# The last chunk of an expert that fills several: high and low row parts side by side as one stationary block

## What is computed

```python
    flat_e = e_idx.reshape(-1)
    order = jnp.argsort(flat_e)
    tok = order // TOP_K
    sizes = jnp.bincount(flat_e, length=N_EXPERTS).astype(jnp.int32)
    xs = t[tok].astype(w_gate.dtype)
    hid = jax.nn.silu(lax.ragged_dot(xs, w_gate, sizes)) * lax.ragged_dot(xs, w_up, sizes)
    y = lax.ragged_dot(hid, w_down, sizes)
```

## Time and profile before

| | us |
|---|---|
| median of 3 runs | 2054.48 |
| lowest and highest | 2053.87, 2055.65 |
| the profiled execution | 2051.71 |
| its span, first to last instruction | 2049.9 |
| PE busy in the span | 1758.5 (86%) |
| DVE busy | 1289.9 (63%) |
| ACT busy | 965.6 (47%) |
| chunks of layer 0, first matmul of the first to first of the last | 680.0 to 1013.2 |
| chunks of layer 1, the same | 1680.2 to 1995.3 |

### The profile page before, as it was taken

The page is one execution under the profiler, slowest core; times in us unless marked ns, Lnnn a source line. Parts: engine busy times, 40 slices in busy tenths (PEclk is TensorE's granted clock), DMA queues, the critical chain, the costliest instruction groups (busy, mean ns, idle before and its releaser), DMA issues. The chain is left out here.

```text
span 2049.9 us, 40296 instructions
## 1 busy us (share of the span) xinstructions
PE 1758.5 (86%) x15365; PEld 1449.2 (71%) x15366; DVE 1289.9 (63%) x1849; ACT 965.6 (47%) x1492; POOL 200.1 (10%) x261
## 2 busy tenths in 40 slices
PE   3998988999697799999919988899996959999992
PEld 0898677788554688888818986888883548888882
DVE  1388255566445796886653882656663368999674
ACT  2254522233312786886432445323332248888651
POOL 0000022222000100000020000212220000000001
PEclk7999999999798899999969999999997979999996
DMA  7221094330323898997642210431004069999854
GB/s 317 72 83 44 9 366 145 129 130 5 72 86 152 311 391 334 345 397 284 227 170 78 77 44 17 163 126 54 2 3 147 31 236 387 402 394 400 351 205 164
DMA packets 112110, 376.64 MB, mean 184 GB/s; under 512 B 14730, under 2 KB 35490, under 8 KB 86374
## 3 DMA queue, kind: packets, MB, share of 16 engines
q1 hardware_dynamic: 83310, 303.85, 39.7%
q10 hardware_dynamic: 20168, 39.89, 5.1%
q0 software_dynamic: 8496, 30.94, 4.0%
HBM read 332.87 MB, written 41.78 MB: 183 GB/s over the span
## 5 line engine op out<-in xcount | busy, mean ns | idle before, releaser
L1967 DVE TENSOR_TENSOR expert_w_lo<-shared,expert_w_hi 128x2048 fp32r<-128x2048 f32 x192 | 430.5, 2285 | 49.2 <-ACT expert_w_hi L1909 48.7
L1909 ACT ACTIVATE expert_w_hi<-shared 128x2048 fp32r<-128x2048 f32 x192 | 361.0, 1915 | 43.8 <-PEq L143 40.6
L1851 PE MATMUL ps<-expert_w_hi,expert_x_hi 128*128 128x512 f32 x592 | 232.0, 392 | 6.3 <-DVE expert_x_lo L1963 6.3
L1853 PE MATMUL ps<-expert_w_hi,expert_x_lo 128*128 128x512 f32 x592 | 231.8, 392 | 0.0
L1852 PE MATMUL ps<-expert_w_lo,expert_x_hi 128*128 128x512 f32 x592 | 231.7, 391 | 0.0
L1851 PEld LDWEIGHTS ps<-expert_w_hi,expert_x_hi 128*128 128x128 f32 x592 | 112.2, 190 | 30.5 <-issue 7.1
L1853 PEld LDWEIGHTS ps<-expert_w_hi,expert_x_lo 128*128 128x128 f32 x592 | 112.0, 189 | 23.4
L1852 PEld LDWEIGHTS ps<-expert_w_lo,expert_x_hi 128*128 128x128 f32 x592 | 112.0, 189 | 23.2
L1887 PE MATMUL ps<-expert_w_hi,expert_hid_hi 128*128 128x512 f32 x296 | 118.7, 401 | 1.0 <-ACT expert_hid_hi L1941 0.2
L1013 POOL TENSOR_TENSOR mixer_NTb<-mixer_Bt,consts_sb 128x256 f32<-128x256 f32 x120 | 88.6, 762 | 282.0 <-DVE mixer_Bt L1288 215.2
L1888 PE MATMUL ps<-expert_w_lo,expert_hid_hi 128*128 128x512 f32 x296 | 115.5, 390 | 0.0
(11 more groups left out here) (342 smaller groups left out, 3700.6 us busy)
## 6 DMA issues: line engine op xcount, KB each, us to landing
shared<-in_w_gate SPq DMA_DIRECT2D x64, 1024.0 KB, 7.2
shared<-in_w_up SPq DMA_DIRECT2D x64, 1024.0 KB, 8.8
shared<-in_w_down SPq DMA_DIRECT2D x64, 1024.0 KB, 9.1
qkv<-in_w_ada SPq DMA_DIRECT2D x20, 1280.0 KB, 6.0
shared<-in_w_in SPq DMA_DIRECT2D x10, 2048.0 KB, 7.9
y_table<-expert_y ACTq DMA_DIRECT2D x37, 512.0 KB, 8.8
qkvT<-in_w_ada SPq DMA_DIRECT2D x20, 768.0 KB, 8.3
y_table<-zero ACTq DMA_DIRECT2D x1, 12800.0 KB, 50.8
```

The source lines that it names most:

```text
L1851: pe.matmul(bank, hi, w_hi[:, j, w], start=first, stop=False)
L1853: return pe.matmul(bank, lo, w_hi[:, j, w], start=False, stop=last)
L1909: act.activation(w_hi[:, j, :], raw[:, j, :], ACT.Copy).then_inc(w_hi_done, 1)
L1967: dve.tensor_tensor(w_lo[:, j, :], raw[:, j, :], w_hi[:, j, :].bitcast(F32), ALU.subtract).then_inc(w_lo_done, 1)
```

## The change

A last chunk with at most 64 rows, of an expert that has others before it, takes a path of its own (`full` is false there). The 64 high and the 64 low parts of its rows are set side by side as one stationary block of 128 (`x_both`), and two products (with `w_hi` and with `w_lo`) take the place of three. The upper and lower halves of the result then have to be added: the gate product by two copies of ACT and an addition of DVE ahead of Silu, the hidden rows by the transposing matmul itself (against two stacked identities, `eye`), the output by two copies of ACT and two additions of DVE. The same is done for the hidden rows (`hc`, a view of `hid_hi`). To make `x_both`, ACT and DVE each make one more instruction in chunks that have another behind them.

Which path is taken is computed in the router (`R.full`, one number for each expert), loaded by a fourth value load of each engine, and tested by two branches: one ahead of the full code, one ahead of the new code. All experts pass these, those with one chunk too.

```diff
@@ tail_phase, PE and DVE
-                for t in range(NT):
-                    for u in range(t + 1):
+                for t in range(NT + 1):
+                    n = min(t + 1, NT)
+                    for u in range(n):
...
+                ch.link(dve.tensor_tensor(tmp2[:, 4, :], G.ps[:, BX, NT * NE:(NT + 1) * NE], tmp2[:, 0, :], ALU.subtract))
+                ch.link(dve.tensor_scalar(tmp2[:, 4, :], tmp2[:, 4, :], float(HC - P), None, ALU.is_gt))
+                dve.scalar_tensor_tensor(out=R.full[:, :], in0=tmp2[:, 0, :], scalar=1.5 * P, in1=tmp2[:, 4, :], op0=ALU.is_lt, op1=ALU.max)
@@ for_experts, all engines
+                full = eng.value_load(R.full[0:1, bass.ds(e, 1)], min_val=0, max_val=1)
...
-                chunk(e, eng.value_load(R.last[0:1, bass.ds(e, 1)], min_val=0, max_val=MAXC - 1), True, final)
+                k = eng.value_load(R.last[0:1, bass.ds(e, 1)], min_val=0, max_val=MAXC - 1)
+                with eng.If(full > 0):
+                    chunk(e, k, True, final, True)
+                with eng.If(full < 1):
+                    chunk(e, k, True, final, False)
@@ expert_phase, PE
+                def half_product(bank, rows, j, w, first, last):
+
+                    pe.matmul(bank, rows, w_hi[:, j, w], start=first, stop=False)
+                    return pe.matmul(bank, rows, w_lo[:, j, w], start=False, stop=last)
...
+                        if not full:
+                            if q % HQ == 0:
+                                pe.wait_ge(h_lo_done, k * 2 + (q // HQ + 1))
+                            for h in range(2):
+                                w = slice(q % 2 * D + h * 512, q % 2 * D + (h + 1) * 512)
+                                mm = half_product(G.ps[:, 5 + h, :], both(hc, q), j, w, q == 0, q == KF - 1)
@@ ACT
-                    act.activation(sg[:, :], G.ps[:, 0, :], ACT.Silu).then_inc(sg_done, 1)
+                    if full:
+                        act.sem_inc(gc_done, 1)
+                    else:
+                        act.activation(sg[lower, :], G.ps[upper, 0, :], ACT.Copy)
+                        act.activation(sg[upper, :], G.ps[lower, 0, :], ACT.Copy).then_inc(gc_done, 1)
+                        act.wait_ge(gs_done, k + 1)
+                    act.activation(sg[:, :], G.ps[:, 0, :] if full else sg[:, :], ACT.Silu).then_inc(sg_done, 1)
...
+                        for h in range(2):
+                            act.activation(y[lower, h * 512:(h + 1) * 512], G.ps[upper, 5 + h, :], ACT.Copy).then_inc(yc_done, 1)
@@ DVE
+                    if full:
+                        dve.sem_inc(gs_done, 1)
+                    else:
+                        dve.wait_ge(gc_done, k + 1)
+                        dve.tensor_tensor(sg[:, :], sg[:, :], G.ps[:, 0, :], ALU.add).then_inc(gs_done, 1)
                     next_lo(0)
...
+                        for h, done in enumerate((ya, yd)):
+                            dve.wait_ge(yc_done, k * 2 + (h + 1))
+                            dve.tensor_tensor(y[lower, h * 512:(h + 1) * 512], y[lower, h * 512:(h + 1) * 512], G.ps[lower, 5 + h, :],
+                                              ALU.add).then_inc(done, 1)
```

More of the change, by code:

```diff
@@ L1766, in expert_phase @@
         y = ph.sb("y", [P, D])
+        xc = ph.sb("x_both", [P, KD, 2, HC], F32R)
+        hc = h_hi[:, :].rearrange("p (q a n) -> p q a n", q=KF, a=2)
         cur = ph.sb("cur_idx", [P, 1], I32)
@@ L1771, in expert_phase @@
             ph.sem(n) for n in "picked g_p u_p xt_p ht_p y_p half_used w_hi_done w_lo_done".split())
-        sg_done, hid_done, x_hi_done, x_lo_done, h_hi_done, h_lo_done, ya, yd, y_out, passed = (
-            ph.sem(n) for n in "sg_done hid_done x_hi_done x_lo_done h_hi_done h_lo_done ya yd y_out passed".split())
+        gc_done, yc_done, gs_done, sg_done, hid_done, x_hi_done, x_lo_done, h_hi_done, h_lo_done, ya, yd, y_out, passed = (
+            ph.sem(n) for n in "gc_done yc_done gs_done sg_done hid_done x_hi_done x_lo_done h_hi_done h_lo_done ya yd y_out passed".split())
         gathered = ph.dma_sem(G.soft["gathered"])
         turned = G.ps[:, 2:4, :].rearrange("p b n -> p (b n)")
+        turned_q = turned.rearrange("p (q n) -> p q n", n=P)
         HQ = KF // 2
+        lower, upper = slice(0, HC), slice(HC, P)
         def half_of(a, m):
@@ L1857, in _, with chunk @@
                 turn(0, 0, KD)
-                def chunk(e, k, last, final):
+                def chunk(e, k, last, final, full):
                     pe.wait_ge(x_lo_done, k + 1)
@@ L1867, in chunk @@
                             at = slice(q * P, (q + 1) * P)
-                            mm = product(G.ps[:, n, :], x_hi[:, at], x_lo[:, at], j, q % 4 * FF, q == 0, q == KD - 1)
+                            if full:
+                                mm = product(G.ps[:, n, :], x_hi[:, at], x_lo[:, at], j, q % 4 * FF, q == 0, q == KD - 1)
+                            else:
+                                mm = half_product(G.ps[:, n, :], both(xc, q), j, slice(q % 4 * FF, q % 4 * FF + FF), q == 0, q == KD - 1)
                             if last and q == 3:
@@ L1902, in _, with take @@
             def _(act):
-                def take(k):
+                def take(k, last):
                     act.wait_ge(xt_p, k + 2)
                     act.wait_ge(u_p, k + 1)
+                    if not last:
+                        act.activation(xc[:, :, 0, :], turned_q[:, :, 0:HC], ACT.Copy)
                     act.activation(x_hi[:, :], turned, ACT.Copy).then_inc(x_hi_done, 1)
@@ L1951, in chunk @@
                     dst = A.y_table.rearrange("(c p) n -> c p n", p=P)[bass.ds(k, 1)].rearrange("a p n -> p (a n)")
-                    act.dma_start(dst, y[:, :]).then_inc(y_out, 16)
+                    n = P if full else HC
+                    act.dma_start(dst[0:n], y[0:n, :]).then_inc(y_out, 16)
                 for_experts(act, chunk)
@@ L1960, in _, with take @@
             def _(dve):
-                def take(k):
+                def take(k, last):
                     dve.wait_ge(x_hi_done, k + 1)
+                    if not last:
+                        dve.tensor_tensor(xc[:, :, 1, :], turned_q[:, :, 0:HC], xc[:, :, 0, :].bitcast(F32), ALU.subtract)
                     dve.tensor_tensor(x_lo[:, :], turned, x_hi[:, :].bitcast(F32), ALU.subtract).then_inc(x_lo_done, 1)
@@ L1971, in _, with chunk @@
                 split(0, 0)
-                take(0)
+                take(0, True)
                 for j in range(1, PIECES):
                     split(0, j)
-                def chunk(e, k, last, final):
+                def chunk(e, k, last, final, full):
                     def next_lo(j):
@@ L1990, in chunk @@
                         dve.wait_ge(h_hi_done, k * 2 + (m + 1))
-                        dve.tensor_tensor(h_lo[:, at], hid_turned(m), h_hi[:, at].bitcast(F32), ALU.subtract).then_inc(h_lo_done, 1)
-                    take(k + 1)
+                        if full:
+                            dve.tensor_tensor(h_lo[:, at], hid_turned(m), h_hi[:, at].bitcast(F32), ALU.subtract).then_inc(h_lo_done, 1)
+                        else:
+                            here = hc[:, m * HQ:(m + 1) * HQ]
+                            dve.tensor_tensor(here[:, :, 1, :], turned_low(m), here[:, :, 0, :].bitcast(F32), ALU.subtract).then_inc(h_lo_done, 1)
+                    take(k + 1, last)
                     for j in range(1, 3):
```

52 lines of the change are left out of this document (38 added, 14 removed).

## The result

| | before | after |
|---|---|---|
| median of 4 runs, side by side on one chip, us | 2055.07 | 2086.47 |
| lowest and highest | 2053.87, 2057.51 | 2081.20, 2088.86 |
| profiled execution, span | 2051.71, 2049.9 | 2086.73, 2085.0 |
| mean granted clock of TensorE | 0.936 | 0.923 |

The ratio is 1.0148, with a 95% interval of 1.0126 to 1.0169: 30 us slower by the ratio, 31 by these medians. The prediction said 13.5 slower, 2068, and at most 2081. The direction was right, the size was not: the time lies above the range.

What follows compares the result with a forecast made beforehand. PE's 18.30 us per expert was taken as the bound, ACT with DVE close behind at 17.97. Terms 11.1 + 4.5 + 0.1 + 2.5 - 3.9 made +14.3, less a little for slack: +13.5, 2068 us, range 2053 to 2081.

Steps and rivals of the forecast that it cites:

- the gain did not come: Rival: border stays hidden and Silu's delay is free, so 27.2 us go: 2027, or 2038 with borders priced; chance 0.09.
- the border was not free: Rival: the border costs nothing, the 11.1 us vanish and about +3 is left, 2057; chance 0.13.
- PE's instructions were not fetched again: Rival: the longer loop no longer fits and is fetched again, +60 to +120 us, 2115 to 2175; chance 0.05.
- the new code was entered: Rival: the new path is never taken, only borders are paid, about +13 us, 2067.5; chance 0.02.
- The border of every one-chunk expert: Between experts: one value load and two branches more, period 18.30 to 18.80 us, +11.1 together over 21 borders.
- the borders around second chunks: Borders ahead of a first chunk of two, and between the two: 0.1 us each, taken as nothing for all.
- The new chunk: Silu at 7.05, hidden rows 13.05, output product 13.8, next chunk at 18.7 us: +0.4 against 18.3, nothing gained.
- The chunk behind it: Full chunk after a new one: late Silu, period 19.6 us, both chunks 38.5 instead of 37.0; +4.5 for three.
- period = Silu + 11.94: Chunk behind a new one: rule from a profiled second chunk, Silu at 7.03 and period 18.97, giving 19.6 us.
- clock term: In new chunks: PE's idle stretch halves its clock for part of the output product; 0.8 us each, +2.5 for four.
- The very last chunk: Expert 15 of layer 1: no pieces behind Silu, output product sooner and shorter, additions take 1.1 back; -3.9 us.
- The router: Five more small matmuls and three more DVE instructions, standing where engines wait: 0, at most 0.5 us each layer.

Runs made afterwards that it cites:

- the kernel with the flag at 1: The whole change, but the router's flag is 1 for every expert, so the new code is never entered; ratio 1.0080, +16.4 us over the kernel before.
- without the addition ahead of Silu: The whole change, but new chunks leave out the addition of the gate's halves and its two copies; ratio 1.0121, +24.9 us over the kernel before.
- the last expert alone: Kernel before, with the new code and its flag only in each layer's last expert; 0.9969 (-6.4 us), again 0.9954 (-9.5 us).
- with the transposes: The whole change, but a new chunk's hidden rows are turned by the other chunks' transpose, their halves not added; ratio 1.0135, +27.7 us over the kernel before.
- one and the same kernel: Kernel before plus only the router's additions (five matmuls, three DVE instructions per layer); ratio 0.9987, and 0.9991 when measured again.
- the branches' 3.7: The whole change, flag not loaded, both branches testing the already loaded last-chunk index, new code never entered; ratio 1.0018, +3.7 us over the kernel before.
- reordering: The whole change, but in new chunks hidden rows go ahead of two weight pieces on ACT and the first on DVE; 1.0160, +32.9 us over the kernel before.

## Why the prediction was wrong in size

*What bounds the experts* was read rightly. ACT's loop holds the experts as closely as PE's, the order on ACT puts pieces ahead of hidden rows, and the 27 us of matmuls saved did not arrive. All four rivals were wrong: the gain did not come, the border was not free, PE's instructions were not fetched again (105 transfers, none in the loops' rounds but the first two), the new code was entered (160 products with `x_both`). The Trainium skill (Runtime: NRT & Kernel Launch, section Instruction fetch mechanics) gives PE room for 2048 instructions; the trace agrees with that in so far as a loop of some 530 (my count) was not transferred again.

*The border of every one-chunk expert*: forecast +11.1, measured +16.4. The mechanism held (both engines show it, side by side), the price did not. ACT's 0.83 us was 0.60 for the load and 0.23 for two branches; its mean border grew by 1.05 (2.63 to 3.68). The three prices are there in the sequencer's rows after the change (the branches again 0.16 and 0.07). Two things were missing: the loop's own jump takes 0.26 us instead of 0.16, and value loads are not of one length. At best one takes 0.27 us, but up to 1.23 in the trace after; the four of a border took 1.29 in the mean, the three before it 0.91, 0.1 more than one load at its usual 0.28. The period became 18.98, where I had 18.80: the loop of 17.97 and the border's 1.05 make 19.02. For PE 0.45 was forecast, and its gap grew by 0.3. The second half of the miss is that I set the borders around second chunks at 0.1 each and took nothing for all. In the kernel with the flag at 1 the full chunk behind one, in layer 0, took 19.73 instead of 18.56 and its follower 19.44 instead of 18.45; they cost about 1 each. In layer 1 it took 21.82 instead of 18.69: two loads of the border ahead of it took 0.88 and 1.15 us, and PE's clock fell in it. That execution was 5 us above the median of its kernel, so not all of this is in the 16.4.

*The new chunk*: forecast 18.7 us to the next one, measured 19.85 to 20.53. Up to Silu the working held (7.4 for 7.05). The step that failed is "hid_hi at 13.05, output product at 13.8": I took the matmul against the doubled unit matrix for a transpose. In fp32 it is two matmuls, 1.0 to 1.2 us for a pair where a pair of transposes is 0.4 to 0.5 (0.6 to 0.7 at the halved clock), and ACT waits for it, as the new chunk's rows show: 0.34, 0.95 and 0.23 us. The halved clock came as forecast, and made the 16 output matmuls 4.4 to 5.3 us from first to last start instead of 3.5.

*The chunk behind it* is where most of the rest went. I forecast 38.5 us for both (the terms, 18.75 and 19.6, make 38.35); they took 42.8, 42.3 and 42.3, against 37 before. Three steps of that sum were short. Silu to Silu, from 7.05 to 26.4, was to be 19.35 and was 21.7. Taken from the rows above: output copies 12.78 us after Silu instead of 11.25 (the three waits on PE, 1.52 together), so the output's transfer at 16.19 instead of 14.75; then 4.01 instead of 3.23 to the table load. For this I had used the border of a one-chunk expert, 2.56. The border that leaves a second chunk was longer already; ACT before the change, at this place:

```profile
1960.51 0.34 ACTq L1952 DMA_DIRECT2D y_table<-expert_y  x1
1963.67 1.28 ACT L1932 ACT_TABLE_LOAD   x1 [2.66 <-issue]
```

3.16 us, and 0.85 on top with the change. Nearly all of the difference to 2.56 is one value load, that of the last chunk's number, here and then in the border of the earlier trace rows:

```profile
L1793 ACTq TENSOR_LOAD <-last_chunk x1: 853/853/853, 1962.6 to 1962.6; - x1
```

```profile
L1793 ACTq TENSOR_LOAD <-last_chunk x1: 277/277/277, 741.8 to 741.8; - x1
```

What makes a load long at one border and not at another was not tried. Last, "period = Silu + 11.94" was read from a chunk whose PE had little to wait for. Now it was Silu + 13.0 to 13.5, since PE waited again and its clock fell a second time. The full chunk behind the new one, with the change (its turn and the window that follows), and then the same chunk without the addition ahead of Silu:

```profile
2004.35 0.65 PE L1866 MATMUL ps<-consts_sb,expert_hid 128*128 128x128 f32 x2 [2.77 <-DVE expert_hid L2054]
```

```profile
2005.30:2008.70 3.40, 3.40 (x13) 2.90 (x12) 2.10 (x4) 2.89 (x4) 1.15 (x2) 0.61 0.21 89
```

```profile
2000.86 0.51 PE L1866 MATMUL ps<-consts_sb,expert_hid 128*128 128x128 f32 x2 [2.22 <-DVE expert_hid L2054]
```

```profile
2001.40:2004.80 3.40, 3.30 (x18) 2.70 (x18) 2.31 (x4) 3.40 (x5) 1.16 (x2) 1.00 0.22 94
```

Where the clock stayed whole the chunk was Silu + 11.94 again, as forecast; where it fell, 1.2 more. So it is in all seven traces that have new chunks in the loops: of 21 chunks behind a new one, six kept the clock and took Silu + 11.9 to 12.3, fifteen lost it and took Silu + 12.9 to 13.6. I had placed a clock term (2.5 us; four times 0.8 would be 3.2) in the new chunk, where it is mostly hidden, and none here, where it is not.

*The very last chunk*: forecast -3.9, measured -0.3. The order of the working was right, and the last expert alone shows 2.5 of it. What I did not see was a table load of 1.28 us in that chunk, which had none before, and that the clock would be halved for the output product (5.1 us for 16 matmuls instead of 3.5). The first alone does not explain the loss: with the transposes, and without the addition, the table load was there, the clock stayed whole and it was 52.0 us to the end, as with the last expert alone. With the transposes the output product started 1.0 us sooner, and at the whole clock it took 1.6 less. Why the load stands there in one form of the code and not in the other, and what made the clock fall, was not tried.

*The router*: 0 forecast, -1.8 and -2.7 measured for one and the same kernel, with 1.0002 at the end of one interval and 0.9999 of the other: nothing, or some 2 us gained, within what can be told. In the second case the border's 16 and the branches' 3.7 are each 2 larger.

The sum by these terms: 16 for the border, some 12 for the three pairs beyond their border (4.5 and 4.2 over the flag at 1 in layer 0, and 1.9 in layer 1, where that kernel's pair has the long loads), 2 for the new chunk without a full one behind it, 0 for the end.

## What to carry to other kernels

When a loop is held by two engines at once, write down the round of each from one fixed instruction to the same in the next pass (here Silu to Silu), with every wait in it. Work taken from one engine and paid with work on the other is then a loss about as large as the lengthening of that other round, and here reordering did not help. A case that is rare should cost the common one nothing: let its test ride on a value that is loaded anyway, behind a branch that only the rare case enters, or put it where the neighbours have slack, as in the last pass.

## What the runs showed of the hardware

- A matmul in fp32 against a matrix of ones and zeros is not priced like a transpose: 40 records for 20 calls, and 1.0 to 1.2 us for two calls, where two transposes take 0.4 to 0.5 at the whole clock and 0.6 to 0.7 at the halved one.
- Two branches on ACT made its border 0.5 us longer in the mean (3.15 for 2.63): 0.16 and 0.07 for themselves, 0.10 for a loop jump that went from 0.16 to 0.26, 0.12 for a bounds check that came with them. The load of one flag made it another 0.5 to 0.7 longer.
- A value load from SBUF into a register took 0.27 us at best on ACT's sequencer, and up to 1.14 (before) and 1.23 (after) at some borders.
- The length of PE's wait did not tell whether its granted clock fell to half. In the chunks behind a new one it stayed whole behind waits of 1.62 to 3.03 us (six of them) and fell behind waits of 1.92 to 4.87 (fifteen). In the very last chunk it fell behind 1.12 (with the change) and stayed whole behind 1.11 (with the transposes).
